# DeltaNet heads: the transpose of a head's output and its gate product moved into the next head

## The reference, cut to what matters

```
q = l2norm(silu(conv(q))) * hd ** -0.5 ; k = l2norm(silu(conv(k))) ; v = silu(conv(v))
a_mat = (k * beta) @ k.T * decay * (1 - eye)          # per chunk
t_mat = inverse of (eye + a_mat)
for each chunk:  v_new = u - w @ state ; o = q' @ state + attn @ v_new ; state = ...
o = rmsnorm(o, norm_g) * silu(z)
```

## Time and profile before

| what | value |
|---|---|
| median of three runs | 2778.62 us |
| the profiled execution | 2780.53 us, of which the span from first to last instruction is 2778.5 us |
| PE busy | 2610.7 us (94% of the span) |
| DVE busy / ACT busy | 1326.4 us (48%) / 868.5 us (31%) |
| DeltaNet heads in the span | from about 83 us to 579 us |
| mean granted TensorE clock | 0.974 of full speed |

### The profile page before, as it was taken

How to read it: one execution, slowest core, us unless ns; L and a number is a source line. 1 busy time by engine, 2 the same in 40 slices (tenths; PEclk the granted TensorE clock), 3 DMA queues, 4 the chain that set the end, 5 groups by cost and what they waited for, 6 DMA issues and landing times.

```text
span 2778.5 us, 33608 instructions
## 1 busy us (share of the span) xinstructions
PE 2610.7 (94%) x11940; PEld 2110.8 (76%) x11940; DVE 1326.4 (48%) x2205; ACT 868.5 (31%) x1605; POOL 75.1 (3%) x54
## 2 busy tenths in 40 slices
PE   7889999889999876998999999999999999999997
PEld 4777777767788553886888878888888888888886
DVE  4766666634344555334444444444444444444444
ACT  4333233323223433224322223222323222323223
POOL 0110011100000000000000000000000000000002
PEclk9999999989999986998999999999999999999999
DMA  4311101112225002521322222222222222222222
GB/s 156 136 55 44 64 30 64 50 65 98 103 101 211 25 31 72 198 91 68 111 96 92 92 93 104 94 104 92 91 91 99 99 92 105 91 92 103 91 95 91
DMA packets 41613, 255.85 MB, mean 92 GB/s; under 512 B 5088, under 2 KB 5344, under 8 KB 13068
## 3 DMA queue, kind: packets, MB, share of 16 engines
q1 hardware_dynamic: 41484, 254.09, 25.5%
HBM read 245.65 MB, written 13.67 MB: 93 GB/s over the span
## 4 chain that ended last, share of the span: by engine, by line
PE 52%; issue 0%; DVE 0%; ACT 0%; DVEq 0%; ACTq 0%
PE bank L222 35%; PE bank L1599 18%; ACT fin_squares L1703 0%; DVE xs L1746 0%; DVE xs L1745 0%; DVE xs L1661 0%; DVEq L1564 0%; ACT fin_rs L1706 0%; ACT L1706 0%; DVE fin_rs L1740 0%; ACTq L1702 0%; DVEq L1725 0%
## 5 line engine op out<-in xcount | busy, mean ns | idle before, releaser
L222 PE MATMUL bank<-h_hi,w_hi 128*128 128x512 f32 x2272 | 917.9, 404 | 30.5 <-DVE w_lo L183 22.4
L222 PE MATMUL bank<-h_lo,w_hi 128*128 128x512 f32 x2272 | 889.9, 392 | 0.0
L222 PE MATMUL bank<-h_hi,w_lo 128*128 128x512 f32 x2272 | 889.0, 391 | 0.0
L183 DVE TENSOR_TENSOR w_lo<-w_raw,w_hi 128x512 fp32r<-128x512 f32 x840 | 556.3, 708 | 433.7 <-ACT w_hi L174 432.0
L174 ACT ACTIVATE w_hi<-w_raw 128x512 fp32r<-128x512 f32 x836 | 488.9, 624 | 742.4 <-PE bank L1599 311.3
L222 PEld LDWEIGHTS bank<-h_hi,w_hi 128*128 128x128 f32 x2272 | 430.0, 189 | 126.6 <-DVE w_lo L183 15.5
L222 PEld LDWEIGHTS bank<-h_lo,w_hi 128*128 128x128 f32 x2272 | 429.0, 189 | 92.0
L222 PEld LDWEIGHTS bank<-h_hi,w_lo 128*128 128x128 f32 x2272 | 430.4, 189 | 86.6 <-issue 3.5
L1599 PE MATMUL bank<-w_hi,g_hi 128*128 128x512 f32 x704 | 277.9, 395 | 0.0
L1599 PE MATMUL bank<-w_lo,g_hi 128*128 128x512 f32 x704 | 277.8, 395 | 0.0
L1599 PE MATMUL bank<-w_hi,g_lo 128*128 128x512 f32 x704 | 277.8, 395 | 0.0
(11 more groups left out here) (281 smaller groups left out, 1966.0 us busy)
## 6 DMA issues: line engine op xcount, KB each, us to landing
w_raw<-in_weights SPq DMA_DIRECT2D x209, 1024.0 KB, 4.8
bias_rows<-bias_row SPq DMA_DIRECT2D x10, 512.0 KB, 7.3
mix_scratch<-head_out SPq DMA_DIRECT2D x16, 256.0 KB
xs<-in_x SPq DMA_DIRECT2D x1, 4096.0 KB, 17.5
out<-xs SPq DMA_DIRECT2D x4, 1024.0 KB, 6.1
x_t<-in_x_t SPq DMA_DIRECT2D x3, 1024.0 KB, 12.0
nsa_tab<-bias_rows SPq DMA_DIRECT2D x6, 448.0 KB, 7.0
h_lo<-mix_scratch SPq DMA_DIRECT2D x1, 2560.0 KB, 10.0
```

What stands on the lines that cost most here:

```text
L183: nc.vector.tensor_tensor(w_lo[:, s, :], raw_quarter(dve_q), w_hi[:, s, :].bitcast(F32), ALU.subtract).then_inc(lo_done, 1)
L222: m = nc.tensor.matmul(PB[pb][:], a[:, s, k], b[:, kt, :], start=(kt == 0 and n == 0), stop=(kt == KT - 1 and n == 2))
```

## The change

The four transposes of `osc` are no longer at the end of head h. They are in head h+1, behind its L585, L591, L592 and two fill steps, ahead of the transposes of v; their target is bank PB[2], which is free then, instead of W[1]. FILL_NORM's ten fill steps stay ten in sum (two ahead, eight behind). The product with `ng` and `zs` (`head_out`) goes into DVE's program of head h+1, behind the scaling of q and k (L773) and ahead of L777. PE's wait for `o_v` ahead of L591 becomes a wait for the last update of the state (`s_v`); the wait for `o_v` now stands where the fill steps first write PB[2] again. SP stores head h-1 behind the loads of head h. Only the sixth head keeps its end as it was. For that, the first head is written out ahead of the loop on PE, ACT and DVE, and the loop runs over heads 1 to 4.

```diff
--- before.py
+++ after.py
@@ -571,10 +571,12 @@
                 link(dve, nc.vector.tensor_tensor(tok[:, :, C_BG, :], tok[:, :, C_BG, :], tok[:, :, C_BETA, :], ALU.mult))
 
 
-            def dn_pe(pe, h, next_units):
+            def dn_pe(pe, h, next_units, first=False, last=False):
                 def bank_read(u):
                     if u < 3:
                         pe.wait_ge(raw_v, 3 * h + u + 1)
+                        if u == 2:
+                            pe.wait_ge(o_v, h + 1)
                     else:
                         pe.wait_ge(z_free, h + 1)
 
@@ -587,15 +589,20 @@
                 m.then_inc(grow_ps, 1)
 
                 pe.wait_ge(sqr_a, 2 * h + 2)
-                pe.wait_ge(o_v, h + 1)
+                if not first:
+                    pe.wait_ge(s_v, (N_CHUNK + 1) * h)
                 nc.tensor.matmul(W[1][:], ones, B["Y"][:], start=True, stop=True).then_inc(norm_ps, 1)
                 nc.tensor.matmul(W[2][:], ones, B["sk"][:], start=True, stop=True).then_inc(norm_ps, 1)
 
                 pe.wait_ge(silu_a, 3 * h + 3)
+                if not first:
+                    fill(2)
+                    pe.wait_ge(osc_v, h)
+                    turn_out(pe, PB[2])
                 for b in range(TB):
                     m = nc.tensor.transpose(W[3][:, b * P:(b + 1) * P], B["vp"][:, b * P:(b + 1) * P], ident)
                 m.then_inc(tr_ps, 1)
-                fill(FILL_NORM)
+                fill(FILL_NORM if first else FILL_NORM - 2)
 
                 pe.wait_ge(qk_n, 2 * h + 2)
                 for b in range(TB):
@@ -671,9 +678,13 @@
                                      start=False, stop=True).then_inc(s_ps, 1)
                     fill(FILL_C)
                 fill(1000)
-                pe.wait_ge(osc_v, h + 1)
+                if last:
+                    pe.wait_ge(osc_v, h + 1)
+                    turn_out(pe, W[1])
+
+            def turn_out(pe, dst):
                 for b in range(TB):
-                    m = nc.tensor.transpose(W[1][:, b * P:(b + 1) * P], B["osc"][:, b * P:(b + 1) * P], ident)
+                    m = nc.tensor.transpose(dst[:, b * P:(b + 1) * P], B["osc"][:, b * P:(b + 1) * P], ident)
                 m.then_inc(o_ps, 1)
 
             def silu_part(act, h):
@@ -757,7 +768,15 @@
                 nc.scalar.activation(rms[:], ssq[:], ACT.Sqrt, bias=eps_t[:], scale=1.0 / HD).then_inc(o_a, 1)
                 act.wait_ge(o_a, h + 1)
 
-            def dn_dve(dve, h, splits, last):
+            def head_out(dve, h, src):
+                dve.wait_ge(stored, 16 * h + STORED2)
+                dve.wait_ge(o_ps, h + 1)
+                dve.wait_ge(zs_a, h + 1)
+                nc.vector.scalar_tensor_tensor(ob[0][:], src[:], ng[:], B["zs"][:], ALU.mult, ALU.mult)\
+                    .then_inc(o_v, 1)
+                dve.wait_ge(o_v, h + 2)
+
+            def dn_dve(dve, h, splits, last, first=False):
                 left = [min(splits, EARLY)]
 
                 def sp_lo(n):
@@ -773,6 +792,8 @@
                     nc.vector.scalar_tensor_tensor(B[dst][:], B[src][:], sc, B[r][:], ALU.mult, ALU.mult)\
                         .then_inc(qk_n, 1)
 
+                if not first:
+                    head_out(dve, h - 1, PB[2])
                 dve.wait_ge(grow_ps, h + 1)
                 link(dve, nc.vector.tensor_tensor(v3(B["m1"][:]), v3(W[0][:]), bc(hp[:, C_GC, :], P), ALU.subtract))
                 step(nc.vector.tensor_tensor(v3(B["D"][:]), v3(B["m1"][:]), c3b(K_ML), ALU.add))
@@ -841,12 +862,8 @@
                 dve.wait_ge(o_a, h + 1)
                 link(dve, nc.vector.reciprocal(rms[:], rms[:]))
                 nc.vector.tensor_tensor(v3(B["osc"][:]), v3(W[3][:]), bc(rms[:], P), ALU.mult).then_inc(osc_v, 1)
-                dve.wait_ge(stored, 16 * h + STORED2)
-                dve.wait_ge(o_ps, h + 1)
-                dve.wait_ge(zs_a, h + 1)
-                nc.vector.scalar_tensor_tensor(ob[0][:], W[1][:], ng[:], B["zs"][:], ALU.mult, ALU.mult)\
-                    .then_inc(o_v, 1)
-                dve.wait_ge(o_v, h + 2)
+                if last:
+                    head_out(dve, h, W[1])
 
             def dn_pool(pool, h):
 
@@ -854,6 +871,10 @@
                     pool.wait_ge(at_a, h + 1)
                     nc.gpsimd.tensor_tensor(v3(LT[:, lv, :]), v3(B["AT"][:]), c3b(K_LV + lv), ALU.mult)\
                         .then_inc(lt_g, 1)
+
+            def store_head(sp, h):
+                sp.wait_ge(o_v, h + 2)
+                sp.dma_start(mix_d[h, :, :], ob[0][:]).then_inc(stored, 16)
 
             @block.sync
             def _(sp):
@@ -869,8 +890,9 @@
                 spread_bias(sp, range(6, DIL_H + NSA_H))
                 for h in range(DN_H):
                     load_units(sp, (16 + 16 * min(h + 1, DN_H - 1) + 12 * (h == DN_H - 1) + AHEAD + 3) // 4)
-                    sp.wait_ge(o_v, h + 2)
-                    sp.dma_start(mix_d[h, :, :], ob[0][:]).then_inc(stored, 16)
+                    if h:
+                        store_head(sp, h - 1)
+                store_head(sp, DN_H - 1)
 
             @block.gpsimd
             def _(pool):
@@ -889,9 +911,10 @@
                 fill(10)
                 cumulate_pe(pe)
                 fill(1000)
-                with repeat(pe, DN_H - 1, (pe_q, 16, "dn_pe quarters")) as h:
-                    dn_pe(pe, h, 4)
-                dn_pe(pe, DN_H - 1, 3)
+                dn_pe(pe, 0, 4, first=True)
+                with repeat(pe, DN_H - 2, (pe_q, 16, "dn_pe quarters")) as i:
+                    dn_pe(pe, i + 1, 4)
+                dn_pe(pe, DN_H - 1, 3, last=True)
 
             @block.scalar
             def _(act):
@@ -902,8 +925,9 @@
                 small_act(act)
                 split_hi(act, 2)
                 silu_part(act, 0)
-                with repeat(act, DN_H - 1, (act_q, 16, "dn_act quarters"), (act_c, TICKS["dn_act"], "dn_act")) as h:
-                    dn_act(act, h, 16, False)
+                dn_act(act, 0, 16, False)
+                with repeat(act, DN_H - 2, (act_q, 16, "dn_act quarters"), (act_c, TICKS["dn_act"], "dn_act")) as i:
+                    dn_act(act, i + 1, 16, False)
                 dn_act(act, DN_H - 1, 12, True)
 
             @block.vector
@@ -919,8 +943,9 @@
                 nc.vector.memset(S[:], 0.0).then_inc(o_v, 1)
                 for _ in conv_steps(dve, 0):
                     pass
-                with repeat(dve, DN_H - 1, (dve_q, 16, "dn_dve quarters"), (dve_c, TICKS["dn_dve"], "dn_dve")) as h:
-                    dn_dve(dve, h, 16, False)
+                dn_dve(dve, 0, 16, False, first=True)
+                with repeat(dve, DN_H - 2, (dve_q, 16, "dn_dve quarters"), (dve_c, TICKS["dn_dve"], "dn_dve")) as i:
+                    dn_dve(dve, i + 1, 16, False)
                 dn_dve(dve, DN_H - 1, 12, True)
```

## The result

| | before | after |
|---|---|---|
| median, four runs each | 2778.41 us (2776.2 to 2779.57) | 2754.28 us (2752.52 to 2757.42) |
| profiled execution | 2780.53 us, span 2778.5 | 2752.52 us, span 2750.4 |

The ratio is 0.9909, with an interval of 0.9896 to 0.9921: 24.1 us less, where 17.2 less were forecast.

The account below looks back on a forecast made before the run. Within each DeltaNet head, the chain through DVE was taken to decide up to the first inversion level, then PE, busy 94% overall. 21.2 us saved at boundaries less 4.0 for the product made 17.2, hence 2761.4 us, range 2756 to 2767.

Parts of the forecast that it names:

- Part 1: At five head boundaries, sums of squares come out from behind the output: 28.4 - 5 x 1.45 = 21.2 us less.
- rival (a): The table load stays in the loop, costing four boundaries 1.2 us each of the gain: 2766.2 us; chance 0.14.
- Part 2: The output product enters DVE's chain between scaled k and L777: 0.8 us, five times, 4.0 us added.
- Part 3: PE's moved transposes and fill steps fit its spare time: nothing added; without spare time, up to 1 us a head.
- Part 4: SP's store no longer holds up the next weight loads: taken as nothing, bounds 0 and 7.9 us.
- (b): The boundary wait only moves to PE's L602, so just the product's 5 x 0.8 is added: 2782.6 us; chance 0.05.
- (d): L602 to L629: PE's clock falls to 1.2 GHz and stays, 6.9 us a head, 2813 us; chance 0.04.
- signs of being wrong: Reciprocal no earlier, new PE wait over 2 us at L602 or L596, longer k to first square, lower clocks 170-200 us.
- the sum: Over the DeltaNet heads, 21.2 - 4.0 = 17.2 us less, giving a median of 2761.4 us.
- Rival (c): Code moves, so ACT's or DVE's loop branches wait for code fetch, three costing 15 us: 2776.4 us; chance 0.04.

Follow-up runs that it names:

- a_load: The changed kernel with a one-element Exp on ACT between head 0 and the loop, so the table load at L740 returns: 2764.12 us, ratio 0.9941.
- a_late: The changed kernel with the output product four steps later in DVE's chain, behind the product with beta (L802): 2752.11 us, ratio 0.9905.
- b_sp: The kernel before with SP's new order alone, a head's store behind the loads of the next: 2781.22 us in one execution.
- a_store: The changed kernel with SP's old order, the store ahead of the next loads: 2787.95 us, ratio 1.0025.
- b_unroll: The kernel before with only head 0 written out ahead of the loop on PE, ACT and DVE, nothing moved: 2776.33 us, ratio 0.9983.
- b_hint: The kernel before with PE's sequencer told of the MLP loop's branch (hint_back_edge=True); the text gives no total time or ratio.
- after_again: The changed kernel, unaltered, timed and profiled once more: 2755.68 us, ratio 0.9908.
- a_late5: The same kernel as a_late, timed in more rounds beside the changed kernel: 2753.66 us, ratio 0.9898.
- a_slot224: The changed kernel with the first instruction of PE's MLP loop placed at slot 224 of a 256-slot code block: 2755.93 us in one execution.
- a_first: The changed kernel with the output product first in DVE's next head, ahead of the copy L787: 2762.73 us in one execution.

## Why the prediction came out as it did

**Part 1, the boundary: right.** Forecast 28.4 - 7.25 = 21.2; measured 28.4 - 7.2 = 21.2. The load went, PE's L591 ran at full clock, and DVE's 0.58 us of idle time at the old loop end did not return. a_load gives the price had it stayed: 1.3 each (rival (a) had 1.2), and the clock's extra at some. That the load goes was the better guess, not something shown: one load in the MLP spoke for it.

**Part 2, the product: right in kind, a little too dear.** 0.8 each forecast; 0.78 measured from k to L798, but 0.65 at the head's end, so 3.2 instead of 4.0. L798 and what follows it are not all on the chain; a_late shows that four steps on, the product costs next to nothing.

**Part 3, PE's order: right.** L609's waits grew from 5.3 to 8.4 us, those for low parts from 7.7 to 12.2, L636's fell from 8.1 to 2.7. PE's lead is used up earlier in the head and the length doesn't notice.

**Part 4, SP: the number right, the picture wrong.** Zero was right for this change as it stands (b_sp). But I treated the edit as one of its own, whose only worth was the waits for weights in the trace of before, at most 7.9 us. a_store shows that it is a condition of Part 2: put the product later and leave the store ahead of the loads, and the whole gain and 7 us more are lost.

With these the heads give 18.0 us by the terms and by both profiles, against 17.2. Rivals (b) and (d) were wrong: the wait did not move to L602 in full, and the clock cost nothing. But (d) was right in kind. A lower clock between 170 and 200 us was among the prediction's signs of being wrong, and it came (0.50 from 188.06 to 191.47, and as long in each of two more heads). It stayed free because it was as short as head 0's had been, 3.41 us.

**The step that failed is the sum, which ended at the DeltaNet section and put the rest of the program at nothing.** The median fell by 6.9 us more than forecast. Of that 0.8 is Part 2, and 5.0 is the MLP, without which the time would have been about 2759 us. The two profiles have 9.2 and 9.1 us in the two stretches that follow, and 28.1 and 24.4 in all; the profiled execution before was 2 us above the median:

- *The MLP, 5.0 us.* Rival (c) had the cause in hand and gave it one sign. I read the branches of 4.7 to 5.0 us as something that could be added elsewhere, not as something that was being paid. I had asked for PE's waits in the MLP of before, and the answer was the 3.9 us of "issue" in 4; the prediction makes nothing of it. A loop whose code moves by a written-out head can lose such gaps as well as get them. b_unroll and b_hint show it from two sides, and the reads of code show what is lost: one of two reads at each of four branches.
- *The start of the dilated heads, 4.2 us.* From the last `osc` to the first dilated output it is 49.5 us before and 45.3 after. Two things differ. The next weights come earlier: ACT starts on them 11.6 us behind the last `osc` instead of 13.0. The kernels with a written-out head have 11.6 to 12.5, the three without (before, b_sp, b_hint) 13.0 to 13.6, so this goes with the written-out head; SP issues the load 0.4 us earlier, and why it takes about 1 us less is open. And before, PE waited 3.03 us for a DVE result at L947 and ran at half clock for 6.8 us around it; after, it waits 1.36 (L972) and the clock stays full there (both have 10.2 us of half clock at the last head's end).

```profile
595.02 0.48 PE L947 MATMUL bank<-cst,dil_lg 128*128 128x128 f32 x1 [3.03 <-DVE dil_lg L977]
```

(kernel before), and the same matmul after:

```profile
575.46 0.33 PE L972 MATMUL bank<-cst,dil_lg 128*128 128x128 f32 x1 [1.36 <-DVE dil_lg L1002]
```

Over the runs the time goes with the halved stretch. The five profiles with none (after, after_again, a_late, a_late5, a_slot224) take 45.3 to 45.8 us. Those with 3.4 us of it take 46.9 to 48.9, those with 6.8 take 49.5 to 49.7. That the earlier landing is what spares PE the longer wait, and this the clock, is only argued: a_load and a_first have the early landing and half clock all the same. So of these 4.2 us no run shows the cause; b_unroll, with the early landing and 3.4 us of half clock, has 2.3 of them.

## What to carry to other kernels

Price a boundary between iterations by the chain, from its last fixed event to its first, and not by PE's idle gap: here the gap was 3.2 us and the boundary worth 4.2. When a step is moved later, move everything that waits for it in an in-order queue behind the work that must not wait; an edit that is worth nothing alone can be the condition of the one beside it. And when code is written out ahead of a loop, look at every later loop in the same program for idle time marked "issue" at its turns: here it vanished without an edit there, and it can presumably appear in the same way.

## What the runs showed of the hardware

- A turn of the long PE loop costs its sequencer 4.7 to 5.1 us in the kernels before and b_sp, with two overlapping reads of code, and PE about 1 us of idle time; in all others it costs the sequencer 3.1 to 3.8 us, with one read, and PE nothing. A hint of the branch or other code ahead of the loop is enough to go from one to the other.
- Half clock for 3.41 us is free where DVE has the chain (67.96 to 68.00 us from k to the square with it, 67.97 without) and costs 0.9 us where it meets one matmul group of the chain (L609 in a_load: 2.07 us instead of 1.16).
- A table load at L740 vanished from the loop in every kernel in which both entries to the loop had the same table, and came back with one instruction ahead of it (a_load). By the Trainium skill ("ScalarE activation tables: per-element evaluation and per-set limits", section "Table sets in the compiler and the runtime") tables are placed block by block; this loop without a load shows that a block can take over the table of those before it, where these agree.
